# Closing LayerNorm shared out anew between three engines, and another order for the last expert blocks

## What is computed

```python
h = _layernorm(DN_ALPHA * x + mix, ln1_g, ln1_b)
y = _layernorm(DN_ALPHA * h + _moe(h, ...), ln2_g, ln2_b)

def _moe(x, ...):          # 4 groups of 8 experts: top-1 group, top-2 experts inside it
    ...
    h = silu(xb @ w_gate[e]) * (xb @ w_up[e])      # 1024 -> 512, for the tokens of expert e
    return (h @ w_down[e]) * w[:, None]            # 512 -> 1024, added to the token's row

def _layernorm(x, g, b):
    mu = mean(x); var = mean((x - mu) ** 2)
    return (x - mu) * rsqrt(var + LN_EPS) * g + b
```

## Time and profile before

| | us |
|---|---|
| timed runs (3), median | 1719.68 |
| timed runs, lowest and highest | 1718.02, 1719.79 |
| the profiled execution, its own time | 1711.8 |
| its span, first to last instruction | 1710.0 |

### The profile page before, as it was taken

The page is one execution under the profiler, slowest core; times in us unless marked ns, Lnnn a source line. Parts: engine busy times, 40 slices in busy tenths (PEclk is TensorE's granted clock), DMA queues, the critical chain, the costliest instruction groups (busy, mean ns, idle before and its releaser), DMA issues.

```text
span 1710.0 us, 22521 instructions
## 1 busy us (share of the span) xinstructions
PE 1642.7 (96%) x9285; PEld 1009.8 (59%) x9286; DVE 661.3 (39%) x1395; ACT 339.4 (20%) x670; POOL 163.9 (10%) x169
## 2 busy tenths in 40 slices
PE   7999999999999999999999999999999999999990
PEld 5556777777777666666688555654444444444440
DVE  1446464544542323232477745551111212121225
ACT  1113222323231221222122000101111111111115
POOL 1000000000002422111000000001111111111110
PEclk9999999999999999999999999989999999999995
DMA  7201121121027445443263443289999999999975
GB/s 229 62 18 24 50 63 50 52 61 50 13 75 210 170 148 172 140 136 112 65 235 125 187 160 136 101 302 390 391 392 377 392 395 391 381 389 396 389 268 203
DMA packets 104410, 337.67 MB, mean 197 GB/s; under 512 B 24378, under 2 KB 68482, under 8 KB 87924
## 3 DMA queue, kind: packets, MB, share of 16 engines
q1 hardware_dynamic: 89572, 276.22, 43.0%
q0 software_dynamic: 13568, 55.78, 10.8%
q10 hardware_dynamic: 1168, 4.23, 0.6%
HBM read 307.90 MB, written 35.51 MB: 201 GB/s over the span
## 4 chain that ended last, share of the span: by engine, by line
PE 91%; DMA 5%; DVE 2%; issue 1%; ACT 1%; POOL 0%; SPq 0%; DVEq 0%; POOLq 0%; ACTq 0%
PE psum L1075 12%; PE psum L1189 10%; PE psum L1515 8%; PE psum L1520 7%; PE psum L1377 6%; PE psum L1392 5%; PE psum L1541 4%; PE psum L1116 4%; PE psum L1547 4%; PE psum L979 3%; PE psum L1228 3%; PE psum L1089 2%; DMA arena<-in_w_up 2%; PE psum L1134 2%; PE psum L1528 2%; PE psum L1123 2%
## 5 line engine op out<-in xcount | busy, mean ns | idle before, releaser
L1075 PE MATMUL psum<-arena 128*128 128x258 f32 x896 | 215.3, 384 | 0.0
L1189 PE MATMUL psum<-arena 128*128 128x344 f32 x576 | 182.3, 458 | 0.0
L1075 PEld LDWEIGHTS psum<-arena 128*128 128x128 f32 x896 | 162.9, 190 | 27.9 <-issue 7.0
L1520 PE MATMUL psum<-arena 128*64 128x512 f32 x320 | 141.6, 595 | 0.0
L1521 PE MATMUL psum<-arena 128*64 128x512 f32 x320 | 141.6, 595 | 0.0
L1515 PE MATMUL psum<-arena 128*128 128x512 f32 x320 | 139.8, 595 | 1.1 <-DVE arena L2552 1.1
L1189 PEld LDWEIGHTS psum<-arena 128*128 128x128 f32 x576 | 103.3, 190 | 52.9 <-issue 11.2
L1515 PEld LDWEIGHTS psum<-arena 128*128 128x128 f32 x320 | 60.0, 190 | 73.6 <-issue 73.2
L1377 PE MATMUL psum<-arena 128*128 128x258 f32 x448 | 99.9, 387 | 0.9 <-ACT arena L1802 0.9
L1392 PE MATMUL psum<-arena 128*128 128x512 f32 x224 | 99.2, 596 | 0.0
L1377 PEld LDWEIGHTS psum<-arena 128*128 128x128 f32 x448 | 86.6, 194 | 14.3 <-issue 1.3
(11 more groups left out here) (394 smaller groups left out, 2125.6 us busy)
## 6 DMA issues: line engine op xcount, KB each, us to landing
arena<-in_w_gate SPq DMA_DIRECT2D x32, 2048.0 KB, 24.7
arena<-in_w_up SPq DMA_DIRECT2D x32, 2048.0 KB, 30.3
arena<-in_w_down SPq DMA_DIRECT2D x32, 2048.0 KB, 30.6
arena<-in_w_in SPq DMA_DIRECT2D x33, 512.0 KB, 5.3
gates<-arena SPq DMA_DIRECT2D x16, 516.0 KB, 6.1
arena<-gates SPq DMA_DIRECT2D x16, 516.0 KB, 6.6
arena<-in_x_prompt SPq DMA_DIRECT2D x16, 512.0 KB, 4.5
arena<-in_w_o SPq DMA_DIRECT2D x1, 4096.0 KB, 17.6
```

What stands on the lines that cost most here:

```text
L1075: ins = mm(psum[:, BANK[name[0]], 0:QT], held, moved, start=(k == 0 and name in ("X1", "V6", "Y5")), stop=(k == 3), skip_group_check=True)
L1189: ins = mm(psum[:, FB + t, 0:SP3], wring[:, u, k, :], xT[:, k, t * SP3:(t + 1) * SP3], start=(k == 0), stop=(k == KD - 1))
L1520: g = mm(psum[0:64, 2, :], xgT[:, xpar, k, 0:64], wg[:, k, :], start=(k == 0), stop=(k == KD - 1))
```

## The change

It has two parts.

1. The last letters of the string in `RANK` are put in another order. Blocks 26 to 31 were h m f m q q; they are f m m h q q. All kinds stay as many as they were, and so does every block's room.
2. The closing norm. The tiles n = 0 and n = 4 (`ON_POOL`) are no longer normalised by VectorE: it makes their variance and reciprocal only, and GpSimd applies the rest in three instructions: (x - mean) * reciprocal, times gain, plus bias, each with a wait for the one before. The moments of tile n = 1 (`OWN_MOMENTS`) are made by VectorE (two `bn_stats`, a `bn_aggr`, a copy of the mean and a change of sign of the variance) and no longer by ScalarE. VectorE's order is now centred(n), variance(n + 1), root(n), finished(n). SyncE stores the tiles in the order 1, 2, 0, 3, 5, 4, 6, 7, 8.

```diff
+        ON_POOL, OWN_MOMENTS = (0, 4), (1,)
+        OUT_ORDER = (1, 2, 0, 3, 5, 4, 6, 7)
...
-        RANK = list(range(FIXED)) + [next(kinds[c]) for c in "hhfmhfmhfmhmhfmhfmhfmhfmhmfmqq"]
+        RANK = list(range(FIXED)) + [next(kinds[c]) for c in "hhfmhfmhfmhmhfmhfmhfmhfmfmmhqq"]
...
-            for n, t in enumerate(LAST[:-1]):
-                sp.wait_ge(f_dve, n + 1)
+            for n in OUT_ORDER:
+                t = LAST[n]
+                if n in ON_POOL:
+                    sp.wait_ge(f_pool, 3 * ON_POOL.index(n) + 3)
+                else:
+                    sp.wait_ge(f_dve, DVE_TILES.index(n) + 1)
...
+            for i, n in enumerate(ON_POOL):
+                pool.wait_ge(f_ready, i + 1)
+                pool.tensor_scalar(v, v, mean9[0:r, t:t + 1], sd9[0:r, t, 0:1], ALU.subtract, ALU.mult).then_inc(f_pool, 1)
+                pool.wait_ge(f_pool, 3 * i + 1)
+                pool.tensor_tensor(v, v, ln2g[0:r], ALU.mult).then_inc(f_pool, 1)
+                pool.wait_ge(f_pool, 3 * i + 2)
+                pool.tensor_tensor(v, v, ln2b[0:r], ALU.add).then_inc(f_pool, 1)
...
+                if n in OWN_MOMENTS:
+                    dve.wait_ge(f_ld[t], F_BASE[t] + 16)
+                    link(nc.vector.bn_stats(bst[0:r, 0, :], v[:, 0:512]))
+                    link(nc.vector.bn_stats(bst[0:r, 1, :], v[:, 512:D]))
+                    link(nc.vector.bn_aggr(mv[0:r, 0, :], bst[0:r]))
+                    link(nc.vector.tensor_copy(mean, mv[0:r, 0, 0:1]))
+                    ts(sd9[0:r, t, 0:1], mv[0:r, 0, 1:2], -1.0, None, ALU.mult).then_inc(var_dve, 1)
...
-            for n in range(NT):
-                centred(n)
-                if n:
-                    finished(n - 1)
-            finished(NT - 1)
+            variance(0)
+            variance(1)
+            root(0)
+            for n in range(1, NT):
+                if n in DVE_TILES:
+                    centred(n)
+                if n + 1 < NT:
+                    variance(n + 1)
+                root(n)
+                if n in DVE_TILES:
+                    finished(n)
```

More of the change, by code:

```diff
@@ L422, in build @@
         g_dve, f_dve, f_out, mom_act = sem("g_dve"), sem("f_dve"), sem("f_out"), sem("mom_act")
+        f_ready, f_pool = sem("f_ready"), sem("f_pool")
+        ON_POOL, OWN_MOMENTS = (0, 4), (1,)
+        ACT_MOMENTS = [n for n in range(NT) if n not in OWN_MOMENTS]
+        DVE_TILES = [n for n in range(NT) if n not in ON_POOL]
+        OUT_ORDER = (1, 2, 0, 3, 5, 4, 6, 7)
         f_ld = x_ld + w_ld
@@ L812, in _ @@
             for c in range(2):
-                sp.wait_ge(f_dve, NT + c)
+                sp.wait_ge(f_dve, len(DVE_TILES) + c)
                 t, half = LAST[-1], slice(c * 512, (c + 1) * 512)
@@ L946, in _ @@
             pool.memset(pad_row, 0.0).then_inc(sums_whole, 1)
+            for i, n in enumerate(ON_POOL):
+                t = LAST[n]
+                r = rows_of(t)
+                v = fin[0:r, t, :]
+                pool.wait_ge(f_ready, i + 1)
[4 more added lines that the diff above has]
+                pool.tensor_tensor(v, v, ln2b[0:r], ALU.add).then_inc(f_pool, 1)
         @block.tensor
@@ L1909, in moments @@
                 act.wait_ge(f_ld[t], F_BASE[t] + 16)
-                if n:
-                    act.wait_ge(mom_act, 2 * n)
+                i = ACT_MOMENTS.index(n)
+                if i:
+                    act.wait_ge(mom_act, 2 * i)
                 nc.scalar.activation(waste[0][0:r], fin[0:r, t, :], ACT.Copy, scale=1.0 / D, accum_out=mean9[0:r, t:t + 1]).then_inc(mom_act, 1)
@@ L1925, in _ @@
             for n in range(NT):
-                if n + 1 < NT:
+                if n + 1 in ACT_MOMENTS:
                     moments(n + 1)
@@ L2659, in _, with variance @@
             link(nc.vector.memset(eps, LN_EPS / ALPHA ** 2))
+            def variance(n):
+                t = LAST[n]
+                r = rows_of(t)
+                v, mean = fin[0:r, t, :], mean9[0:r, t:t + 1]
+                if n in OWN_MOMENTS:
[5 more added lines that the diff above has]
+                    ts(sd9[0:r, t, 0:1], mv[0:r, 0, 1:2], -1.0, None, ALU.mult).then_inc(var_dve, 1)
+                else:
+                    dve.wait_ge(mom_act, 2 * ACT_MOMENTS.index(n) + 2)
+                    stt(out=sd9[0:r, t, 0:1], in0=mean, scalar=mean, in1=sq9[0:r, t:t + 1], op0=ALU.mult, op1=ALU.subtract).then_inc(var_dve, 1)
             def centred(n):
@@ L2665, in centred, with root @@
                 v = fin[0:r, t, :]
[L2666 to L2669, removed]
+                stt(out=v, in0=v, scalar=mean9[0:r, t:t + 1], in1=ln2g[0:r], op0=ALU.subtract, op1=ALU.mult).then_inc(g_dve, 1)
+            def root(n):
+                t = LAST[n]
+                r = rows_of(t)
+                dve.wait_ge(sd_act, NT + n + 1)
+                ins = nc.vector.reciprocal(sd9[0:r, t, 0:1], sd9[0:r, t, 1:2])
+                if n in ON_POOL:
+                    ins.then_inc(f_ready, 1)
+                else:
+                    link(ins)
             def finished(n):
@@ L2675, in finished @@
                 v = fin[0:r, t, :]
-                dve.wait_ge(sd_act, NT + n + 1)
-                link(nc.vector.reciprocal(sd9[0:r, t, 0:1], sd9[0:r, t, 1:2]))
-                dve.wait_ge(g_dve, n + 1)
+                dve.wait_ge(g_dve, DVE_TILES.index(n) + 1)
                 for part in ((slice(0, 512), slice(512, D)) if n == NT - 1 else (slice(0, D),)):
                     stt(out=v[:, part], in0=v[:, part], scalar=sd9[0:r, t, 0:1], in1=ln2b[0:r, part], op0=ALU.mult, op1=ALU.add).then_inc(f_dve, 1)
-            for n in range(NT):
-                centred(n)
-                if n:
-                    finished(n - 1)
-            finished(NT - 1)
+            variance(0)
[9 more added lines that the diff above has]
+                    finished(n)
 INS = ["x_prompt", "x_sample", "cache_ckv", "cache_krope", "state_conv", "page_table", "w_in", "conv_w", "q_norm_g",
```

## The result

The changed kernel is slower: 1722.7 us median of 18 runs against 1717.5 us of 18 runs of the kernel before beside it, ratio 1.0040 with the 95% interval 1.0029 to 1.0051, or +6.9 us (the two medians are 5.2 us apart). The prediction had 1714.8 us and faster. The time lies in its wide range (1712.8 to 1725.5) and outside that of the forecast itself (1712.8 to 1717.6); the sign is the other one. The profiled execution of the changed kernel took 1721.79 us, with a span of 1720.0.

The account below looks back on a forecast made before the run. Two serial stages after TensorE's last long products were taken as the bound in reach: the last adds (-1.6 us) and VectorE's closing norm (-3.3). Sum -4.9 from 1719.7 gave 1714.8 us, range 1712.8 to 1717.6, wide range 1712.8 to 1725.5.

Parts of the forecast that it names:

- Part 2: Closing norm: seven large tiles on VectorE at 2.72 us spacing, ending at 1703.6 against 1706.9, -3.3 us.
- the wait of 0.6 for ScalarE: Closing norm: before the variance of n = 6 VectorE catches up with ScalarE's moments and waits 0.6 us.
- the short last tile: End of closing norm: the last tile holds no neighbour's first step, taking 2.8 us where it was 4.2.
- All of this takes it that VectorE's instructions last beside GpSimd's what they last alone: Closing norm: assumption under the forecast that GpSimd's steps don't lengthen VectorE's, large steps staying at 1.28 us.
- VectorE waits for GpSimd: Closing norm rival: GpSimd's steps hold VectorE's up, +10.4 to 10.9 us, time 1725.7 us; chance 0.22.
- The rival's price: VectorE's loss per GpSimd tile in that rival: 6.0 us less some 0.5, 11 us for both tiles.
- Part 3: GpSimd's tiles in the closing norm: 6.3 us each, with 2 us of cover before late stores move the end.
- Part 1: Adds of the last blocks: issue +1.1, block 28's add -2.3, block 29's -0.4, sum -1.6 us.
- TensorE's last product then ends where it did, near 1666.5: Last blocks: TensorE's end stays put, ahead of block 30's add at about 1666.6, so the adds' gain shows.
- the argument about late issues: Last weights: loads issued 5 to 12 us later still find four matrices queued ahead, so they land as before.
- Were that matrix to land 2 us later, 1 us would come back: Last block's up matrix: little cover for the adds' gain; landing 2 us later costs 1 us.
- The last rival: The string of adds doesn't shorten, 96-row add 12 us or last matrices late: 1717.1 us; chance 0.15.

Follow-up runs that it names:

- e4: New closing norm in the old block order, GpSimd's three steps per tile replaced by three memsets, against the kernel before: single time 1714.93 us.
- e10: New closing norm, old block order, gain and bias for VectorE in PSUM, variance with one input tensor, against the kernel before: ratio 0.9990.
- e12: The changed kernel with gain and bias in PSUM, one-input variance and tile 6 stored ahead of tile 4, against the kernel before: ratio 0.9988.
- e9: New closing norm in the old block order, VectorE's large steps reading gain and bias from PSUM, against the kernel before: ratio 1.0008.
- e1: The kernel before with the new order of the last blocks alone, against the kernel before: ratio 0.9997.
- e7: The kernel before with the weight loads of blocks 30 and 31 issued later; profiled, last up matrix landing 535.3 us after the first wide gate product.
- e6: The new block order alone, with block 26's add writing 64 of its 128 rows; one profile, TensorE's wait 5.0 us.
- e11: New closing norm, old block order, gain and bias in PSUM, one-input variance, tile 6 stored ahead of tile 4, against the kernel before: ratio 0.9982.

## Why the prediction was wrong, by its steps

**Part 2 (the closing norm on VectorE, -3.3 us): right.** With GpSimd's reads gone, VectorE ended 26.5 us after the first load, where it had been 29.8 (e4), and 27.1, 26.4 and 26.5 in e10 to e12. The spacing of 2.72 us, the moments of n = 1, the wait of 0.6 for ScalarE (0.7 in e4) and the short last tile came as worked out.

**The sentence that failed first** is "All of this takes it that VectorE's instructions last beside GpSimd's what they last alone". It failed by 9.6 us. I gave the forecast that rests on it 0.45 on the strength of the earlier trace rows, where GpSimd's instructions make descriptors, and had written myself that a large GpSimd step beside a large VectorE step is in no row. The rows could not speak for it. The rival "VectorE waits for GpSimd" is what happened. That 1722.7 lies in the wide range is no merit of the forecast: the range was drawn to take in this rival. The Trainium skill (SBUF — State Buffer, "Who interferes with whom") had it in the prediction as a rule, and adds there that a VectorE instruction with at most one SBUF input, outside the modes that use two ports, doesn't contend, and that a GpSimd instruction that only writes does not hold one with two: e9, e10 and e4 agree, with 1.28 against 3.37, 0.27 against 2.29, and 1.28 beside the memsets. It calls the shared ports an exclusive lock, and says of VectorE's two-port modes that whoever issues first holds them for the whole instruction. The prediction took this for the pair at hand too. Of GpSimd's two-input steps it is nearly so here (2.1 of 2.35 us), of its one-input steps it is not (0.6 to 0.9 of 4.8 us), and there the measurement decides. With a rule that named this pair of instructions and no row against it, this was the likelier case and deserved more than 0.22.

**The rival's price** was 6.0 us a tile, 1.3 + 2 x 2.36, less 0.5; measured 4.8. Two errors nearly cancel. A one-input step of GpSimd lasts 3.79 alone, outside my bounds of 0.9 to 2.36, since the nearest rows were of other operations; but it holds VectorE only 0.6 in the changed kernel. A two-input step holds it 2.1 of its 2.35. Together -3.3 + 9.6 less the vanished wait of 0.6 is 5.7; measured 5.5.

**Part 3 (GpSimd 6.3 us a tile, 2 us of cover)** was mis-sized: 8.6 us a tile alone, 11.4 with VectorE in the way. It thought of the stores behind tile 4 and of nothing else behind GpSimd. What stands behind GpSimd's last instruction is its drain of 8.5 us, which the trace of the kernel before showed, ending at 1683.57 and harmless. Worth 1.5 us after, and with the exclusion taken away the drain eats all of part 2's 3.3 in the profiles of e10 to e12. No rival had it.

**Part 1 (-1.6 us): the first add right, the second and the cover wrong.** Block 28's add was issued 0.8 us later than in the kernel before, from the first wide gate product (+1.1 said), and landed in 10.9 us in e1 (10.8 said). Block 29's took 7.2 (5.8 said, 8.0 the outer end): +1.0 and not -0.4. The sentence that failed is "TensorE's last product then ends where it did, near 1666.5": the argument about late issues is right (e7), but the last matrices land 2.7 us later all the same, and TensorE stands 5.2 to 5.9 us. "Were that matrix to land 2 us later, 1 us would come back" had the place and not the size. The last rival named a cause, the rows of the full block that go out earlier; e6 shows it for a third of the delay at most, and the rest stays open. Over all profiles the first load comes 556.0 to 556.5 us after the first wide gate product with the new order and 553.9 to 558.4, mean 556.2, with the old one (11 profiles): the order is worth nothing, steadier though it is. The timed pairs agree: 0.9997 for e1, 0.9988 beside 0.9982, 0.9977 beside 0.9985.

**The sum**: +5.5 for VectorE, +1.5 for the drain, 0 for the order: +7.0 in the profiles, where the timed runs have +6.9 by the ratio and +5.2 by the medians. Two slips stand beside it. The forecast started from 1719.7, the median of three runs, and that of 18 is 1717.5. And by its own terms, half a microsecond included, its range ends at 1718.1 and not at 1717.6.

**Open.** The ratios of e10, e11 and e12 are all below 1, by 1.7 to 3.1 us, and e11's interval leaves out no change, though the traces of all three show the end of the program where it was. Whether that is the profile or chance isn't settled. What GpSimd does in the 8.5 us of its drain no run shows. Why a one-input step of GpSimd holds VectorE so briefly isn't either. How the old order comes to two rhythms, with the add of block 28 anywhere from 524.2 to 531.0 us after the first wide gate product, was not tried.

## What to carry to other kernels

Before work is moved to an idle engine, ask what its operands pass through together with its neighbour's, and settle that with one small kernel rather than with rows of other operations: here a copy of two vectors into PSUM and a variance by scalars took away the 9.6 us that VectorE lost. Ask too what stands behind the engine's last instruction, for an engine that has long been idle hides its own shutdown. And where transfers are issued tens of us before they land, a later issue can cost nothing: here 11.3 us later changed no landing. What does set the landing needs a mark close to the change, for a far one brings its own scatter.

## What the runs showed of the hardware

- GpSimd's closing drain ended 8.49 to 8.51 us after its last instruction in all seventeen profiles of this case, whether this was a memset of one column (0.1 us) or a step over 128x1024.
- GpSimd's one-input step over 1024 columns takes 3.79 us, its two-input one 2.35, over 8 rows as over 128; over 640 columns 2.51 and 1.54. The one with less to read, which does two operations where the others do one, is the slower.
- Exclusion costs both sides: two-input steps of GpSimd grow from 2.35 to 3.2 and 3.3, and VectorE's lose 2.1, even where they read one column.
- VectorE's two-input step takes 1.27 to 1.28 us with its second input in PSUM, as in SBUF.
- After 5.25 us of waiting TensorE ran at half its clock. The windows of the kernel after (us, busy time and instructions of PE, PEld, DVE, ACT, POOL, granted clock, DMA share, GB/s):

```profile
1658.00:1662.00 4.00, 0.00 (x0) 0.00 (x0) 0.00 (x0) 0.00 (x0) 0.00 (x0) 0.85 0.52 196
1662.00:1665.00 3.00, 2.66 (x28) 1.49 (x32) 0.00 (x0) 0.00 (x0) 1.42 (x1) 0.50 0.53 193
1665.00:1669.00 4.00, 4.00 (x56) 2.26 (x52) 0.00 (x0) 0.37 (x1) 0.00 (x0) 0.67 0.35 117
```

TensorE had no work in the first window. Then the granted clock is 0.50, the lower of its two levels (1.2 GHz), and the 64 products take 6.26 us where they took 3.66 behind the shorter wait. So 2.6 us of the new order's loss on TensorE is the clock and not the matrix. The first window also shows that the DMA engines are busy only 0.52 of the time while TensorE waits for its last big matrix, so the bytes still to be moved are not all that sets its landing.
